# A fifth slot for rounded weights during the first block's feed-forward nets

## The reference, cut to what matters

```python
def first_block(x, ...):
    x = layer_norm(x, ln_in_g, ln_in_b)
    for l in range(DEPTH):                                  # DEPTH = 2
        proj = jnp.einsum('bsd,de->bse', x, w_in[l])
        ...                                                 # three kinds of attention, gates
        mix = jnp.einsum('bsd,de->bse', merged, w_out[l])
        x = layer_norm(DN_ALPHA * x + mix, ln1_g[l], ln1_b[l])
        gu = jnp.einsum('bsd,df->bsf', x, w_ffn_in[l])      # D_FF = 2816
        hidden = jax.nn.silu(gu[..., :D_FF]) * gu[..., D_FF:]
        ffn = jnp.einsum('bsf,fd->bsd', hidden, w_ffn_out[l])
        x = layer_norm(DN_ALPHA * x + ffn, ln2_g[l], ln2_b[l])
    return x

def reference(...):
    return second_block(first_block(...), ...)
```

## Time and profile before

| | us |
|---|---|
| median of 3 runs | 1454.12 |
| lowest and highest run | 1453.71, 1455.78 |
| the profiled execution, whole | 1453.56 |
| its span, first to last instruction | 1452.3 |
| TensorE busy in the span | 1436.5 |
| DVE, ACT, POOL busy | 1040.3, 813.9, 64.5 |

### The profile page before, as it was taken

One profiled execution on the slowest core, in us unless ns is written; L12 is line 12 of the kernel. 1 busy time (PEld: TensorE's weight loads), 2 busy tenths in 40 slices (PEclk: granted clock), 3 DMA queues, 4 the chain that ended last, 5 costly groups with the idle time before them and its releaser, 6 DMA issues.

```text
span 1452.3 us, 19721 instructions
## 1 busy us (share of the span) xinstructions
PE 1436.5 (99%) x7721; PEld 1209.0 (83%) x7721; DVE 1040.3 (72%) x1423; ACT 813.9 (56%) x1177; POOL 64.5 (4%) x100
## 2 busy tenths in 40 slices
PE   7999999999999999999999999999999999999999
PEld 6788878888888888887888888788888888888888
DVE  5766876855557556875865556877988868788886
ACT  6465654455443565754454444676655657765563
POOL 1010000000001000000000000210000012000000
PEclk9999999999999999999999999999999999999999
DMA  8654644565665554642756565436556644456651
GB/s 298 221 191 147 207 141 160 172 219 177 201 207 188 164 188 150 208 154 88 252 182 218 187 201 174 145 106 214 172 186 201 218 130 163 135 182 199 196 187 58
DMA packets 172684, 261.09 MB, mean 180 GB/s; under 512 B 9520, under 2 KB 111568, under 8 KB 172336
## 3 DMA queue, kind: packets, MB, share of 16 engines
q1 hardware_dynamic: 171296, 255.18, 53.8%
q0 software_dynamic: 1152, 4.65, 0.9%
q10 hardware_dynamic: 144, 0.01, 0.0%
HBM read 256.66 MB, written 1.05 MB: 177 GB/s over the span
## 4 chain that ended last, share of the span: by engine, by line
PE 91%; DVE 5%; ACT 1%; DMA 1%; POOL 1%; issue 1%; SPq 0%; DVEq 0%; ACTq 0%
PE ps L458 16%; PE ps L534 11%; PE ps L536 11%; PE ps L535 11%; PE ps L459 9%; PE ps L428 7%; PE ps L432 6%; PE ps L430 6%; PE ps L461 2%; DVE wlo L1714 1%; PE ps L835 1%; PE ps L486 1%; DMA gate<-in_lam 1%; PE ps L638 1%; DVE bn L1721 1%; PE ps L1076 1%
## 5 line engine op out<-in xcount | busy, mean ns | idle before, releaser
L1714 DVE TENSOR_TENSOR wlo<-raw,whi 128x2048 fp32r<-128x2048 f32 (+1 forms) x234 | 519.5, 2229 | 216.2 <-ACT whi L1192 216.2
L1192 ACT ACTIVATE whi<-raw 128x2048 fp32r<-128x2048 f32 (+1 forms) x234 | 434.4, 1865 | 139.5 <-PE ps L536 52.0
L458 PE MATMUL ps<-xT,whi 128*128 128x512 f32 x1008 | 356.5, 395 | 0.0
L459 PE MATMUL ps<-xT,wlo 128*128 128x256 f32 x1152 | 311.2, 280 | 0.0
L534 PE MATMUL ps<-whi,xT 128*128 128x512 f32 (+3 forms) x640 | 250.4, 391 | 3.3 <-DVE wlo L1714 1.8
L536 PE MATMUL ps<-whi,xT 128*128 128x512 f32 (+3 forms) x640 | 242.0, 378 | 0.0
L535 PE MATMUL ps<-wlo,xT 128*128 128x512 f32 (+3 forms) x640 | 241.2, 377 | 0.0
L458 PEld LDWEIGHTS ps<-xT,whi 128*128 128x128 f32 x1008 | 189.0, 188 | 42.3
L459 PEld LDWEIGHTS ps<-xT,wlo 128*128 128x128 f32 x1152 | 217.4, 189 | 6.1
L534 PEld LDWEIGHTS ps<-whi,xT 128*128 128x128 f32 x640 | 120.3, 188 | 26.3 <-issue 6.5
L536 PEld LDWEIGHTS ps<-whi,xT 128*128 128x128 f32 x640 | 120.2, 188 | 22.5
(11 more groups left out here) (244 smaller groups left out, 1965.9 us busy)
## 6 DMA issues: line engine op xcount, KB each, us to landing
raw<-in_w_in SPq DMA_DIRECT2D x120, 512.0 KB, 4.7
raw<-in_w_ffn_in SPq DMA_DIRECT2D x88, 512.0 KB, 4.9
raw<-in_w_up SPq DMA_DIRECT2D x88, 512.0 KB, 4.8
raw<-in_w_ffn_out SPq DMA_DIRECT2D x44, 512.0 KB, 4.4
raw<-in_w_down SPq DMA_DIRECT2D x44, 512.0 KB, 4.5
raw<-in_w_branch SPq DMA_DIRECT2D x24, 512.0 KB, 4.8
raw<-in_w_out SPq DMA_DIRECT2D x16, 512.0 KB, 4.2
raw<-in_w_o SPq DMA_DIRECT2D x16, 512.0 KB, 4.7
```

The costliest lines, as they stand in the source:

```text
L458: PE.matmul(ps[:, b, :], hi, m.xT[:, kt], start=kt == 0, stop=False)
L459: mm = PE.matmul(ps[:, b, 0:S], lo, m.xTh[:, kt], start=False, stop=False)
L1192: AC.activation(m.whi[:, i % SPLIT, 0:w], m.raw[:, slot, 0:w], ACT.Copy).then_inc(s.w_hi, 1)
L1714: DV.tensor_tensor(m.wlo[:, i % SPLIT, 0:w], m.raw[:, slot, 0:w], m.whi[:, i % SPLIT, 0:w].bitcast(F32), ALU.subtract).then_inc(s.w_lo, 1)
```

## The change

A fifth slot of rounded weights, `xhi` and `xlo`, is laid over the last 2048 columns of the two halves of `proj`. From the first piece of each net of the first block to the third piece behind it, every fifth piece goes there, and the others rotate through the four old slots. `rounding_slots` lists for every piece its slot and the piece that had it before, which is what ACT waits for. In this stretch roundings and remainders then stand one piece further ahead in the written order.

```diff
+def rounding_slots(pieces, first, after):
+
+    spans = [(first[1, L, "up", 0], after[1, L, "dn", NSTEP - 1] + 3) for L in range(DEPTH)]
+    slots, last, turn = [], {}, 0
+    for i in range(pieces):
+        slot = SPLIT
+        if not any(a <= i < b and (i - a) % (SPLIT + 1) == 0 for a, b in spans):
+            slot, turn = turn % SPLIT, turn + 1
+        slots.append((slot, last.get(slot)))
+        last[slot] = i
+    return slots
+def weights_of(k, i):
+
+    slot = k.slots[i][0]
+    return (k.m.xhi[:], k.m.xlo[:]) if slot == SPLIT else (k.m.whi[:, slot], k.m.wlo[:, slot])
...
+        ends = [at["proj"] + 4 * (PROJ * (half + 1) - PIECE) for half in range(2)]
+        more = [nc.alloc_sbuf_tensor_at(name, [P, PIECE], F32R, offset=o) for name, o in zip(("xhi", "xlo"), ends)]
...
-            if i >= SPLIT:
-                AC.wait_ge(s.w_used, i - SPLIT + 1)
-            AC.activation(m.whi[:, i % SPLIT, 0:w], m.raw[:, slot, 0:w], ACT.Copy).then_inc(s.w_hi, 1)
+            if k.slots[i][1] is not None:
+                AC.wait_ge(s.w_used, k.slots[i][1] + 1)
+            AC.activation(weights_of(k, i)[0][:, 0:w], m.raw[:, slot, 0:w], ACT.Copy).then_inc(s.w_hi, 1)
...
         for i in (3, 4):
-            catch(1, L, "w", i)
-        catch(1, L, "w", 5)
+            catch(1, L, "w", i, ahead=SPLIT + 1)
+        catch(1, L, "w", 5, ahead=SPLIT + 1)
         turn_hi(0)
-        catch(1, L, "w", 6)
+        catch(1, L, "w", 6, ahead=SPLIT + 1)
...
-        split_to(later + 2)
+        split_to(later + 3)
         if L + 1 < DEPTH:
             turn_hi_quarter(0, 0)
-            split_to(later + 3)
+            split_to(later + 4)
             turn_hi_quarter(0, 1)
-            split_to(later + 4)
         else:
             AC.wait_ge(s.par, 80)
-            turn_hi_gains(0, 0, 16)
-            split_to(later + 3)
-            turn_hi_gains(0, 1, 16)
+            for n4 in range(2):
+                turn_hi_gains(0, n4, 16)
...
-        catch(1, L, "w", 3)
+        catch(1, L, "w", 3, ahead=SPLIT + 1)
         up0 = k.first[1, L, "up", 0]
-        catch(1, L, "w", 4)
+        catch(1, L, "w", 4, ahead=SPLIT + 1)
         DV.wait_ge(s.ln_in, 32 * (L + 1))
         apply(0)
-        catch(1, L, "w", 5, ahead=SPLIT - 1)
+        catch(1, L, "w", 5, ahead=SPLIT)
         turn_lo(0)
-        split_to(up0 + 2)
+        split_to(up0 + 3)
         catch(1, L, "w", 6, ahead=0)
...
-        split_to(later + 1)
+        split_to(later + 2)
         add_down(0, (1, L, "dn", NSTEP - 1))
...
         if L + 1 < DEPTH:
             turn_lo_quarter(0, 0)
-            split_to(later + 2)
+            split_to(later + 3)
             turn_lo_quarter(0, 1)
-            split_to(later + 3)
+            split_to(later + 4)
         else:
-            split_to(later + 2)
             DV.wait_ge(s.par, 80)
             for n4 in range(2):
                 turn_lo_gains(0, n4, 16)
+            split_to(later + 3)
         add_down(1, (1, L, "dn", NSTEP - 1))
         for n4 in range(2):
             stats(1, n4)
-        split_to(later + 3 + (L + 1 < DEPTH))
         apply(1)
```

More of the change, by code:

```diff
@@ L70 @@
 Sems = namedtuple("Sems", SEMS)
-Tensors = namedtuple("Tensors", [n for n, _, _ in SBUF] + ["ps", "down", "cw", "sgw", "brow", "xTh", "xTl"])
-Kernel = namedtuple("Kernel", "nc t out m s raws leads free size first after call bank halves seen")
+Tensors = namedtuple("Tensors", [n for n, _, _ in SBUF] + ["ps", "down", "cw", "sgw", "brow", "xTh", "xTl", "xhi", "xlo"])
+Kernel = namedtuple("Kernel", "nc t out m s raws leads free size first after call bank halves seen slots")
 class Count(defaultdict):
@@ L145, in build @@
     with ExitStack() as ctx:
-        sb = [ctx.enter_context(nc.sbuf_tensor(name, shape, dt)) for name, shape, dt in SBUF]
+        sb, at = [], {}
+        for name, shape, dt in SBUF:
+            at[name] = nc.sbuf_base
+            sb.append(ctx.enter_context(nc.sbuf_tensor(name, shape, dt)))
+        ends = [at["proj"] + 4 * (PROJ * (half + 1) - PIECE) for half in range(2)]
+        more = [nc.alloc_sbuf_tensor_at(name, [P, PIECE], F32R, offset=o) for name, o in zip(("xhi", "xlo"), ends)]
         ps = ctx.enter_context(nc.psum_tensor("ps", [P, 8, 512], F32))
@@ L151, in build @@
                     flat[:, 0:NSTEP * 16].rearrange("p (c f k) -> p c f k", c=NSTEP, f=4),
-                    flat[:, D:2 * D].rearrange("p (h q) -> p h q", h=8), flat[:, 2 * D:2 * D + 640], named["xT"][:, :, 0, :], named["xT"][:, :, 1, :])
+                    flat[:, D:2 * D].rearrange("p (h q) -> p h q", h=8), flat[:, 2 * D:2 * D + 640], named["xT"][:, :, 0, :], named["xT"][:, :, 1, :], *more)
         s = Sems(*[ctx.enter_context(nc.semaphore(name)) for name in SEMS])
         k = Kernel(nc, t, out, m, s, (s.raw0, s.raw1, s.raw2), (s.lead0, s.lead1, s.lead2), (s.free0, s.free1, s.free2), size, first, after, call,
-                   {}, [], {})
+                   {}, [], {}, rounding_slots(len(size), first, after))
         tensor_program(k)
@@ L410, in gemm @@
             w = c * width * len(outs(0))
-            views.append([x[:, (i0 + i) % SPLIT, 0:w].rearrange("p (k n w) -> p k n w", k=c, w=width)
-                          for x in (m.whi, m.wlo)])
+            views.append([x[:, 0:w].rearrange("p (k n w) -> p k n w", k=c, w=width) for x in weights_of(k, i0 + i)])
         for th in ths:
@@ L444, in by_features @@
             for kt in range(8):
-                slot, j, end = (i0 + kt // 4) % SPLIT, kt % 4, kt == 7
+                i, j, end = i0 + kt // 4, kt % 4, kt == 7
                 before(pair, kt)
@@ L450, in by_features @@
                     o, b = j * 2 * FC + f * P, f ^ first
-                    hi, lo = [x[:, slot, o:o + P] for x in (m.whi, m.wlo)]
+                    hi, lo = [x[:, o:o + P] for x in weights_of(k, i)]
                     if not joined:
@@ L522, in half @@
         for i, count in enumerate(kts):
-            hi, lo = [x[:, (i0 + i) % SPLIT, 0:count * width].rearrange("p (k w) -> p k w", k=count)
-                      for x in (m.whi, m.wlo)]
+            hi, lo = [x[:, 0:count * width].rearrange("p (k w) -> p k w", k=count) for x in weights_of(k, i0 + i)]
             if th == 0:
@@ L1151, in last_down @@
             i = k.first[2, L, "dn", c]
-            hi, lo = [x[:, i % SPLIT, :].rearrange("p (k n w) -> p k n w", k=2, n=2) for x in (m.whi, m.wlo)]
+            hi, lo = [x.rearrange("p (k n w) -> p k n w", k=2, n=2) for x in weights_of(k, i)]
             for b, o in enumerate(narrow(1)):
@@ L1503, in scalar_program @@
         turn_hi(1)
-        split_to(up0 + 4)
+        split_to(up0 + 5)
         up_in_half(0, 0)
@@ L1713, in split_to @@
             DV.wait_ge(s.w_hi, i)
-            DV.tensor_tensor(m.wlo[:, i % SPLIT, 0:w], m.raw[:, slot, 0:w], m.whi[:, i % SPLIT, 0:w].bitcast(F32),
+            hi, lo = weights_of(k, i)
+            DV.tensor_tensor(lo[:, 0:w], m.raw[:, slot, 0:w], hi[:, 0:w].bitcast(F32),
                              ALU.subtract).then_inc(s.w_lo, 1)
@@ L2177, in vector_program @@
         turn_lo(1)
-        split_to(up0 + 3)
+        split_to(up0 + 4)
         hidden_half(0)
-        split_to(up0 + 4)
+        split_to(up0 + 5)
         hidden_half(1)
@@ L2207, in vector_program @@
             features_out(c, 0)
-            split_to(k.after[up] - 1 + SPLIT)
+            split_to(k.after[up] + SPLIT)
             features_out(c, 1)
@@ L2211, in vector_program @@
             if c < NSTEP - 1:
-                split_to(k.after[up] + SPLIT)
+                split_to(k.after[up] + SPLIT + 1)
             features_lo(c)
             if c < NSTEP - 1:
-                split_to(k.after[1, L, "dn", c - 2] + SPLIT)
+                split_to(k.after[1, L, "dn", c - 2] + SPLIT + 1)
         later = k.after[1, L, "dn", NSTEP - 1]
-        split_to(later + 1)
+        split_to(later + 2)
         add_down(0, (1, L, "dn", NSTEP - 1))
```

6 lines of the change are left out of this document (3 added, 3 removed).

## The result

| | before | changed |
|---|---|---|
| median | 1453.75 us (10 runs) | 1457.03 us (10 runs) |
| lowest and highest | 1453.49, 1455.78 | 1456.37, 1460.67 |
| profiled execution | 1453.56 | 1456.46 |
| its span | 1452.3 | 1455.1 |

The ratio is 1.0023, with a 95% interval of 1.0016 to 1.0031: slower, by 3.3 us of the medians and 2.9 us of the two profiled executions. The forecast was 1456.3, within a range of 1453.0 to 1458.3.

A forecast was written before the change was run, and what follows sets the result against it. TensorE, busy 1436.5 of 1452.3 us, was taken as the bound, so only net entries and exits count: +3.7 - 0.6 - 0.6 = +2.5 us, giving 1456.3 us, with an 8-in-10 range of 1453.0 to 1458.3.

The forecast's parts named there:

- Entry, layer 2: Start of layer 2's net: remainder ahead of the second eviction waits for a late load, delaying `apply(1)` and TensorE; +3.7 us.
- Entry, layer 1: Start of layer 1's net: the new remainder fits before the second eviction, 0.2 us ahead of it; 0 us.
- How the wait divides: Layer 2's entry: TensorE loses about 2.4 us at the first half's turns, the rest at the second's; 4 us and more total.
- Exit, layer 1: End of layer 1's net: without `wlo` beside it POOL's step shortens, `apply(1)` comes earlier, the split limits the gain; -0.6 us.
- Exit, layer 2: End of layer 2's net: `add_down(1)` 1.25 us later, POOL 1.9 us shorter, so `apply(1)` comes earlier; -0.6 us.
- POOL's long step: Both exits: POOL's first step, 2.12 us beside the `wlo`, is shut out by it and falls to 0.19 us.
- the root: Layer 2's exit: POOL's root for the next projection, beside the moved remainder, comes some 1.3 us later and costs nothing.
- Rival 2: POOL's long step is its own: exit 1 gives 0, exit 2 costs 1.25 us; 1459.0 us, chance 0.06.
- Inside the nets: Within both nets: no rounding is ever late, so working a piece further ahead changes nothing; 0 us.
- Rival 1: Layer 2's entry: load in time, 0.8 us or less instead of 3.7; 1453.1 us, chance 0.13.
- Rival 3: Layer 2's entry: load lands later still, or TensorE's gaps cost beyond their length; +3.5 to +5 us, chance 0.08.
- Rival 4: The net itself gains, or the edit undoes more than seen; faster by over 2.9 us, chance 0.03.

The follow-up runs named there:

- e2: Changed kernel with layer 2's entry in its old order, the additional piece caught up in the net's third chunk; 1453.14 us.
- e1: Changed kernel with layer 2's parameter loads issued behind the first two pieces of the net instead of ahead; 1453.37 us.
- e4: Changed kernel: parameters later, only `up0` early at entries, fifth slot restricted within nets, layer 2's exit remainder between the two groups of splits; 1451.06 us.
- e11: e4 with the places of `xhi` and `xlo` exchanged; 1450.71 us.
- e3: Changed kernel with both exits back in their old order, the rest as changed; 1458.58 us.
- e10: e1 with `xhi` placed 128 bytes lower and `xlo` left in place; 1452.32 us.
- e6: Changed kernel with one more load of 512 KB ahead of layer 2's net; 1459.03 us.

## Why the prediction was right, and where it was not

**Entry, layer 2 (+3.7): the mechanism as written, the size within its bounds.** `xhi` started at 708.37 behind a DMA (said: 708.6), the eviction at 712.53 (712.8), and `apply(1)` moved from 724.27 to 727.65. TensorE was 0.37 us late there already, so the term is 727.65 - 724.27 - 0.37 = +3.0 us in this execution. The step that missed is the landing, which I took at the same time as before, 708.61. It came at 708.35, so that `xhi` started 0.28 us ahead of the 708.65 said, on a TensorE that was 0.37 us later, and these two make up the 0.65. SP issued this DMA at 702.88 and not at 701.01, so from issue to landing it took 5.5 us and not 7.6: the time of the landing stayed nearly the same and the duration did not, so the bounds, which were made by changing the duration, rested on the wrong one of the two. By medians the term is larger: undoing the entry (e2) gives 3.9 us, mending the load (e1) 3.7, where the table gives 2.9 to 3.0 for either. Whether a later landing or the clock makes up the rest is not shown. Nor does the spread of the runs tell: it is 4.3 us for the changed kernel and 1.0 for e4, but 2.6 for e11, which has the load in time as well, and 2.3 for the kernel before.

**Entry, layer 1 (0): right.** TensorE was 0.59 us late ahead of it and 0.62 us behind it, and the second eviction still waits for TensorE, by 0.25 us (0.2 was said):

```profile
262.73 0.69 DVE L1891 SCALAR_TENSOR_TENSOR x<-x,ps 128x512 f32<-128x512 f32 x1 [0.25 <-PE ps L558]
```

**How the wait divides: mis-sized.** I expected 2.4 us at the turns of the first half; it was 0.56 + 0.79, and 1.52 + 0.25 at the second. Together that is 3.1 us, where "4 us and more" was to be the sign. The turn at the first half was not late before, and had about 1.7 us of slack: `apply(0)` came 3.0 us later as seen from TensorE, and made it wait 1.35. That changes nothing in the sum, since TensorE waits at the last turn for the rest.

**Exit, layer 1 (-0.6): right.** The half product that follows started at 473.65 against 473.46, on a TensorE that came 0.92 us late: -0.73 there, and -0.56 measured at 486.4. That the second turn would no longer be late, and that the split of the first quarter would be what TensorE waits for next, came true: the wait is now 0.37 us for the split and none for `x`. (The 0.87 us said to be at stake do not follow from the two times beside them, 473.46 and 472.3, which are 1.16 us apart; since the split bounds the gain, the term is the same.)

**Exit, layer 2 (-0.6): right, -0.8 to -0.9.** `add_down(1)` came 914.47 - 909.64 - 3.70 = 1.13 us later (said: 1.25), `apply(1)` 3.72 us behind it (3.75), so `apply(1)` is 0.80 us earlier. I had seen the moved remainder eat the first relief, but not that it could be placed in ACT's shadow (e4).

**POOL's long step.** Shown: 0.19 us at both exits, 2.12 us again in e3. The rule of the Trainium skill ("SBUF — State Buffer", section "SBUF: two separate sides"), by which a two-input DVE instruction and a GpSimd instruction that reads SBUF shut each other out for their whole length, agrees with every row here, and with the 2.28 us of the root beside the moved remainder. Seen from TensorE it ends 1.0 us later than before (1.3 was said). In e4 the remainder has run since 905.74 when the root starts, at 907.50; the root takes 0.58 us, to 908.08, and the remainder ends at 908.02. The root was said to cost nothing, and nobody waited for it. Rival 2 is out.

**Inside the nets (0): wrong by 0.3 us each.** I looked at waits only, and there are none. The step that failed was to take products as equally long wherever their weights lie. Two thirds to three quarters of the loss are in the distances with the new slot (0.23 of 0.34 us in net 1, 0.22 of 0.29 in net 2), the rest in the others, and with `xhi` 128 bytes lower neither is left (e10). That the place does it is shown, by one test; by what mechanism is not. The same drift, 0.34 to 0.37 us over net 1, stands in the table for the changed kernel, e1, e2 and e3.

**The other rivals.** Rival 1, the load in time, was not the case; e1 is the kernel that it describes, and has 1453.4 us where rival 1 said 1453.1. Rival 3 was not the case in the profiled execution, but e6 shows how near it was: with 0.7 us more of waiting than the longest wait of the changed kernel the clock fell. Rival 4, a gain in the nets, is out: they lost.

**The sum** was +2.5 and is +3.3 by medians, +2.9 in the traces: +3.0 at the entry (3.7 to 3.9 by medians), +0.7 in the nets, -0.6 and -0.9 at the exits, and 0.6 of scatter at the start of the trace. The scatter is no part of the change; without it the traces are +2.3 apart. That this is so near to +2.5 is partly luck: the entry came out some 0.7 us below its term and the nets 0.7 us above theirs. I put 0.63 on "within 0.2%" and 0.34 on "slower", and it is slower, just over that bound. An error of 0.8 us in a sum of four terms was to be expected, and a forecast of +2.5 against a bound of 2.9 should have had the two nearly even.

## What to carry to other kernels

Before you let an engine work further ahead, ask of each instruction that moves forward whether its data is there by then: a load that lands late is invisible as long as its reader comes later still, and the issue order of the loads has to move with the reader. When the order of loads, the place in an in-order list and a shared port each decide between some tenths and some 3 us, the same added buffer is worth -3 or +3 us; use it only at the places where somebody waited. And place the remainder where another engine's step is being awaited anyway, and never beside a POOL step on the critical chain.
